# Head 0 of a DeltaNet layer: key norms ahead of the decay exponentials on ScalarE, key products behind four projection chunks, three unread products in place of nine

## What is computed

```python
hp = modulate(rms_norm(xp, g_norm1[layer]), mod_p[0], mod_p[1])
proj = h @ w_in
qkv = silu(depthwise_conv(proj[..., :QKV_DIM], conv_w))
beta = sigmoid(gates[:, :, 0])
g = -exp(a_log) * softplus(gates[:, :, 1] + dt_bias)
q, k = l2_norm(q), l2_norm(k)
# in each chunk of 64 tokens, and direction:
gc = cumsum(g)
decay = where(incl, exp(gc[:, None] - gc[None, :]), 0)
m = where(strict, (k * beta) @ k.T * decay, 0)
tmat = inverse(eye + m)
w, u = tmat @ (k * beta * exp(gc)), tmat @ (v * beta)
```

## Time and profile before

| | us |
|---|---|
| median of three runs | 1579.98 |
| lowest and highest | 1578.20, 1583.39 |
| profiled execution, in all | 1586.21 |
| its span in the trace | 1584.0 |
| TensorE busy | 1442.6 (91%) |
| VectorE busy | 807.4 (51%) |
| ScalarE busy | 474.6 (30%) |
| GpSimd busy | 201.6 (13%) |

### The profile page before, as it was taken

How to read it: one execution, slowest core, us unless ns; L and a number is a source line. 1 busy time by engine, 2 the same in 40 slices (tenths; PEclk the granted TensorE clock), 3 DMA queues, 4 the chain that set the end, 5 groups by cost and what they waited for, 6 DMA issues and landing times.

```text
span 1584.0 us, 34040 instructions
## 1 busy us (share of the span) xinstructions
PE 1442.6 (91%) x14714; PEld 1016.4 (64%) x14714; DVE 807.4 (51%) x1586; ACT 474.6 (30%) x1066; POOL 201.6 (13%) x201
## 2 busy tenths in 40 slices
PE   3999989999999998778898999988989999999994
PEld 2555567745588886556676776766755444788883
DVE  1278678734443433535566665665644525343432
ACT  2201655512100000544554544554531202000000
POOL 2200020100312121131011010110100002112111
PEclk9999999999999999889998998999999999999998
DMA  9764573232899999522101201111012433999994
GB/s 344 263 224 134 171 244 123 79 120 102 294 344 345 338 342 352 160 72 56 45 22 46 64 22 46 45 42 59 6 57 74 156 106 142 318 341 344 338 291 112
DMA packets 165158, 268.68 MB, mean 170 GB/s; under 512 B 7697, under 2 KB 107289, under 8 KB 164337
## 3 DMA queue, kind: packets, MB, share of 16 engines
q1 hardware_dynamic: 149008, 206.29, 38.5%
q0 software_dynamic: 16000, 60.23, 13.0%
HBM read 237.45 MB, written 36.36 MB: 173 GB/s over the span
## 4 chain that ended last, share of the span: by engine, by line
PE 75%; DVE 9%; issue 5%; DMA 4%; ACT 3%; DVEq 1%; SPq 1%; POOL 0%; ACTq 0%; POOLq 0%
PE psum L1679 14%; PE psum L928 9%; PE psum L2125 8%; PE psum L1690 7%; PE psum L580 5%; PE psum L2187 4%; PE psum L2137 2%; PE psum L334 2%; PE psum L2684 2%; PE psum L1392 2%; PE psum L489 2%; PE psum L1671 2%; PE psum L944 2%; DMA arena<-in_w_mod 1%; PE psum L955 1%
## 5 line engine op out<-in xcount | busy, mean ns | idle before, releaser
L2125 PE MATMUL psum<-hT,ring 128*128 128x384 f32 (+1 forms) x736 | 241.9, 453 | 1.0 <-ACTq L213 0.7
L2125 PEld LDWEIGHTS psum<-hT,ring 128*128 128x128 f32 x736 | 128.3, 194 | 34.5 <-issue 2.1
L1679 PEld LDWEIGHTS psum<-arena,ring 128*128 128x128 f32 x1152 | 131.1, 192 | 12.4 <-issue 10.4
L1679 PE MATMUL psum<-arena,ring 128*128 128x128 f32 x1152 | 131.9, 275 | 4.8 <-DVE arena L1720 4.8
L1758 DVE TENSOR_TENSOR arena<-arena,psum 128x256 f32<-128x256 f32 x34 | 14.3, 421 | 211.7 <-PE psum L1679 211.7
L737 DVE SCALAR_TENSOR_TENSOR arena<-arena,params_sb 128x655 f32<-128x655 f32 x120 | 106.1, 906 | 5.6
L2187 PEld LDWEIGHTS psum<-arena 32*32 32x32 f32 x5120 | 55.7, 111 | 65.3 <-issue 37.6
L2187 PE MATMUL psum<-arena 32*32 32x32 f32 x5120 | 64.9, 200 | 29.6 <-issue 18.5
L1620 POOL DMA_INDIRECT ysum<-arena,small x34 | 53.9, 1587 | 285.5 <-DVE arena L1728 284.9
L1741 ACT ACTIVATE arena<-psum 128x256 f32<-128x256 f32 x34 | 13.1, 384 | 222.6 <-PE psum L1679 222.6
L928 PE MATMUL psum<-ring,arena 128*128 128x512 f32 x160 | 72.6, 608 | 1.0 <-ACTq L213 1.0
(11 more groups left out here) (476 smaller groups left out, 2626.8 us busy)
## 6 DMA issues: line engine op xcount, KB each, us to landing
arena<-in_w_mod SPq DMA_DIRECT2D x18, 1024.0 KB, 5.2
ring<-in_m_w_gate SPq DMA_DIRECT2D x18, 1024.0 KB, 11.2
ring<-in_m_w_up SPq DMA_DIRECT2D x18, 1024.0 KB, 16.8
ring<-in_m_w_down SPq DMA_DIRECT2D x18, 1024.0 KB, 15.1
ring<-in_w_mod SPq DMA_DIRECT2D x17, 1024.0 KB, 5.5
modN<-in_m_w_down SPq DMA_DIRECT2D x16, 1024.0 KB, 15.9
ring<-in_c_w_in SPq DMA_DIRECT2D x24, 512.0 KB, 6.7
arena<-in_m_w_gate SPq DMA_DIRECT2D x8, 1024.0 KB, 13.6
```

What stands on the lines that cost most here:

```text
L1679: m = pe.matmul(bank((2, 4)[half] + (1, 3)[half] * q, P, f * P), gu_slot[s][:, c0:c0 + P], xgT[:, q, k, :], start=(k == 0), stop=(k == KC ...
L2125: m = pe.matmul(bank(un % 2, w), ring[:, s, c0k:c0k + P], hT[:, k, o:o + w], start=(k == 0), stop=(k == KC - 1))
```

## The change

Three edits. In `gates_pe` three unread products stand in place of nine. In `heads_pe` head 0's key products move from behind chunk 39 to behind chunk 35 of the projection. In `heads_act` the copies of unit 2, the key norms and the copies of unit 3 move ahead of the ten distances, and the decay exponentials (`decays`) go behind the key features.

```diff
--- before.py
+++ after.py
@@ gates_pe
-            unread_products(pe, 9)
+            unread_products(pe, 3)
             pe.wait_ge(S("mod_raw"), 6)
@@ heads_pe
             kn_to_features(0)
-            project(0, 32, 40)
+            project(0, 32, 36)
             key_products(0)
-            project(0, 40, 48)
+            project(0, 36, 48)
@@ heads_act
             silu(0, 0, kf)
-            distances(0, 0, 10)
-            decays(0)
             take_unit(0, 2)
             key_norms(0)
             take_unit(0, 3)
+            distances(0, 0, 10)
             key_features(0)
+            decays(0)
             take_unit(0, 4)
```

## The result

The changed kernel takes 1572.64 us (median of 11 runs, 1566.17 to 1579.5) against 1579.99 us before (11 runs, 1576.87 to 1589.43). The ratio, estimated over all runs, is 0.9943 with a 95% interval of 0.9926 to 0.996; it need not be that of the two medians, 0.9953. The medians differ by 7.35 us where 6.4 were forecast, 1572.6 against 1573.6. A later comparison gave 0.9956 (0.9937 to 0.9974), 1574.55 against 1582.01. Single runs of one kernel spread over ten us and more. So steps of a few us are read from the traces, as distances between two instructions, and the times only carry the sum.

What follows compares the result with a forecast made beforehand. TensorE, 75% of the chain, was taken to bound the kernel: shortening the chain before the eight heads shortens the run. Terms -3.5 - 4.1 + 1.2 = -6.4 us took 1579.98 to 1573.6, range 1570.0 to 1578.3.

Steps and rivals of the forecast that it cites:

- Edit 1: Norm stage, three unread products for nine: VectorE's first modulation begins 3.5 us earlier, 1.6 lost to VectorE's own scaling.
- Edit 2: Head 0's new order on ScalarE and TensorE: VectorE's transition, released by GpSimd's masks, comes 4.1 us earlier.
- the split at four chunks: Head 0's projection on TensorE: key products behind four chunks instead of eight bring nothing, both end ahead of GpSimd's masks.
- The moved pause: TensorE still 5.5 us before head 0's block products, then 4.35 us at the lower clock: costs 1.2 us, bounds 0 and 3.3.
- Rival A: The pause eats head 0's gain, lower clock over the first levels: sum -4.3 or about -3 us; chance 0.24.
- rival B: No clock price for the pause, luckier fall in the norm stage: -7.6 us, 1572.0 down to 1570; chance 0.24.
- C: Edit 2 holds but Edit 1 gives nothing, a load or ScalarE holding the first modulation: -2.9 us, 1577.1; chance 0.06.
- The norm stage's clock: The clock's fall there may come sooner with fewer products; counted 0, bounds -1.5 (fall misses the tail) and +3 us.
- Rival D: Unread products kept the clock up; without six, key projections and block products run slower: +2.1 us, 1582.1; chance 0.04.
- The rule of the Trainium skill on transposes: Speaks against cutting plain products ahead of the norm stage's transposes; by it the time would be 1582.1.

Runs made afterwards that it cites:

- the run with eight: Changed kernel with head 0's key products back behind eight projection chunks of unit 4 instead of four: transition 22.00 us behind the first projection, ratio 0.9959 to before.
- the run with the products only: Kernel before with three unread products in place of nine, head 0's order as before: ratio 0.9981 (0.9964 to 0.9999) to before.
- The run with head 0 alone: Changed kernel with the nine unread products restored, so only head 0's new order differs from before: ratio 0.9975 (0.996 to 0.999) to before.

## Why the prediction was right, and where not

- **Edit 1** was put at 3.5 us, by VectorE's own scaling as the floor. Measured 3.62 in the trace, 3.0 (0.2 to 5.7) in time. Fewer than three products are worth nothing more, as the floor says, and no load took the wait's place. What the prediction did not have is the wait for the decay rows in head 0, 0.9 us, which this edit alone also takes away.
- **Edit 2** was put at 4.1 us, with GpSimd releasing the transition. Against the trace before, 4.34 to 4.36 was measured in every trace of the order, released by GpSimd. The transition stood at 21.99 behind the first projection where the steps gave 22.2; most of that is the key features, which end 0.62 behind the distances instead of 0.75. Of the 4.35, 0.9 is the wait for the decay rows, which stands in the earlier trace rows and was not named in the prediction; with three products in both kernels the order is worth 3.47. The claim that the split at four chunks is worth nothing is shown by the run with eight.
- **The moved pause**, +1.2 us: the fall came, its length after the restart was 4.4 us (forecast 4.35), and its own price was 1.2 to 2.2, so the 1.2 was at the low end. But the term as a whole had the wrong sign. The stretch behind the block products did not get longer than before, it got shorter: 27.2 to 28.2 against 30.70, or against 28.8 in the run with the products only. Two things were missed. In the old order, too, the clock falls there. In the trace before it did so from 736.0 for 3.4 us. In the run with the products only it did so at 707.0, behind a pause of 2 us that I had called free on the strength of one trace. So both orders pay for a fall, and the +1.2 was no difference between them. And the stalls of 1.45 and 3.45 us in the two traces of the old order became 0 to 1.04 in those of the new one; why is open, as said above. Rival A, which put this price at 3.3 and stood at 0.24, is refuted by every trace of the order.
- **The sum.** Read with the ratio, -9.0 us (-11.7 to -6.3) and in the second comparison -7.0 (-10.0 to -4.1), the gain lies between the forecast's -6.4 and rival B's -7.6 or beyond. Both intervals hold both numbers, so the times do not choose between them; the medians' -7.35 is nearer to B and outside the -5.2 to -7.0 that had the chance of 0.42. The first interval shuts out A's -4.3 and C's -2.9, the second only C's. B's reason, no price for the pause, is false as told, since the fall was paid for; but the kernel before paid for one too, so the difference of the two is about none, as B's sum has it. The time is inside the stated range with a term of the wrong sign in the sum, and this is luck in part. The spans agree by luck too. Of the 13.0 us that the profiled kernel gains between the copy L659 and the key convolution, 3.2 are lost ahead of it and 3.0 behind it, where nothing was changed. The block products started at 705.02 for a forecast of 704.6 because the 3.2 of late start and the 2.5 of the next point nearly cancel.
- **The norm stage's clock.** In the trace before it fell at 661.0 and 674.6; in twelve of the thirteen later traces it did neither on the path (25.8 us from the modulation to the projection, 28.28 before); one fell at 672.8 (27.51). The run with head 0 alone has the nine products and no such fall (25.90). So the 2.5 us between the two profiled executions is where the fall happened to lie, not something that the change needs. I had bounded this luck at 1.5. How often the falls come with nine products the two traces of it do not say, so a share of it may belong to the change. Rival D (the products kept the clock up) is refuted: with none of them the only fall was in VectorE's stage. (D's sum has a slip: 5.4 us doubled is 10.8, not 10.3; it decides nothing.) The rule of the Trainium skill on transposes (TensorE: Matmul & The Clock Gate, Part 4: PE-mode transpose), that the full clock does not engage for them, does not decide the time here. The traces do not agree with it: the transposes behind three products ran at the full clock, 1.06 for eight. Where the clock did fall, with no products, it was after a wait of 3.42 us and cost nothing.

## What to carry to other kernels

When two chains meet in one instruction, shortening one is worth only what lies down to the other. List both ends before pricing the edit; the next edit is then the other chain (here the masks, 1.4 to 1.9 us, and the order of the exponentials, 0.6). Look for every wait that an edit takes away, also a small one for a transfer: two edits can take away the same one, and then their gains do not add. A longer pause of TensorE brought a fall of the clock with it here, and a few wide unread products in it took that back in the traces. But count instructions too, since many small products in the pause ran into stalls. A single trace's clock falls are partly place and luck: read the whole stretch in both kernels, and compare distances between two instructions over several traces, before a fall is counted as cost or as free.

## What the runs showed of the hardware

- TensorE in a run of small products: 95 of 32 x 32 (190 records) ran in 1.80 us, then it stood for 3.37 with no releaser in the profile, then 64 ran in 1.29 and it stood for 2.99. One more stall of 1.52 came in the block products behind them. Behind a pause of 5.8 us the block products and what follows had 0 to 1.04 us of such stalls in 27 to 28 us.
- GpSimd's product of 128 x 640 took 1.95 us with VectorE's product of the same shape beside it and 1.31 to 1.32 in every other place; VectorE's took 0.82 to 0.83 either way.
- The granted clock fell at the end of a pause of 2 us in one trace (707.0, products only) and not in another of the same order at that place (710.2 to 712.2 in the earlier trace rows), where it fell at 736.0.
- One small write to memory (L1917) landed after 3.6 and 3.7 us with nine products in the norm stage and after 1.5 in twelve traces with three or none; the cause is open.
